# Combining the experts' sums: stores on ScalarE's queue, one addition moved to GpSimd, one semaphore for four loads

## The chip, the cores and the metric

The kernel runs on one core of a Trainium2 chip. The metric is the time of the kernel on the device in microseconds; the time before is 1642.48 us, the median of three runs. All numbers of the trace come from one profiled execution.

## What is computed

One step of a one-layer diffusion trunk on 128 context tokens and 1024 latent tokens of 1024 values: a modulated norm, one projection, linear attention and windowed attention, an output projection with a residual, then a mixture of 64 small experts (8 for each token) with one shared expert, a gated residual and a final norm. The change touches only the end of it:

```
h = silu(einsum('td,edf->tef', xt, wg)) * einsum('td,edf->tef', xt, wu)
routed = einsum('tef,efd->td', h * gates[..., None], wd)
...
xl = xl + g2 * moe(...)          # the gated residual; moe = routed + shared
y_sample = rms_norm(xl, final_norm_g)     # and y_prompt from xc
```

## The kernel before

The program is a row of stages, each in a block of its own, with one instruction stream for each engine: `project`, `linear_attention`, `window_attention`, `out_and_route`, `experts` and `combine`. All values are float32. The 1152 tokens are held as 9 tiles of 128 tokens (`NT`), tile 0 being the context; `x1` keeps the 9 residual tiles of 128x1024 in SBUF from `out_and_route` to the end.

The stage `experts` works in blocks of token rows that share an expert and adds each block's rows into one of two DRAM arrays, `sum_rows0` and `sum_rows1`, each with two halves of rows. So the routed output of a tile is the sum of four 128x1024 blocks in DRAM: `i % 2` picks the array, `i // 2` the half.

The stage `combine` begins when every engine has left `experts`. It handles tile after tile:

- SP issues the four loads of a tile (512 KB each) into `sums[:, t % NB, i, :]`, a ring of `NB` = 6 tiles, in the order 2, 3, 0, 1 (`ARRIVE`), each with a semaphore of its own (L2235). From tile 6 on it first waits until TensorE and DVE are done with the tile that held the slot. After tile 1 it also loads the final norm's weights, `fg`. The stores of the nine results follow in a second loop of the same queue, each after `out_done` (L2241).
- TensorE adds by multiplying with the identity and accumulating in PSUM: all four blocks of the low 512 columns into `ps_low` (L2255), and blocks 0 and 1 of the high 512 columns into `ps_high` (L2252). It takes each load as it comes. A matmul in the code stands as two instructions in the trace.
- VectorE (DVE) adds blocks 2 and 3 of the high columns (L2265), adds `ps_high` to that (L2268), multiplies both halves by the gate row `g2` (L2270, L2272) and adds the product to `x1` (L2274). Then it does the norm of the tile before: the reciprocal (L2280) and the scaling with `rstd` and `fg`, which is written back in place to `x1` (L2282).
- ScalarE (ACT) makes the sum of squares (L2298) and its root (L2300).
- GpSimd (POOL) has nothing to do in this stage.

The order on every engine is the order of the code; nothing reorders it. The set of engines that may read a tile is bounded by the semaphores `low_done`, `g_done`, `x_done`, `ssq_done`, `std_done` and `out_done`.

Of the kernel before, what the change touches and what calls it, by code (L numbers as in the profile page):

```python
# [5 lines left out]
F32 = mybir.dt.float32  # L6
BF16 = mybir.dt.bfloat16
I32 = mybir.dt.int32
ALU = mybir.AluOpType
ACT = mybir.ActivationFunctionType  # L10
AX = mybir.AxisListType

P = 128
D = 1024
KD = D // P
NT = 9
# [20 lines left out]
def cond_of(t):  # L37

    return 0 if t == 0 else 1
# [2157 lines left out]
def combine(nc, dram, keep):  # L2197

    with ExitStack() as ctx:
        def sb(name, shape, dt=F32):  # L2200
            return ctx.enter_context(nc.sbuf_tensor(name, shape, dt))

        def sem(name):
            return nc.alloc_semaphore(name)

        H = D // 2
        NS = 4
        NB = 6
        sums = sb("sums7", [P, NB, NS, D])
        r = [sb(f"r7_{i}", [P, D]) for i in range(2)]  # L2210
        fg = sb("fg", [P, D])
        junk = sb("junk7", [P, D])
        ssq = sb("ssq7", [P, NT])
        std = sb("std7", [P, NT])
        rstd = sb("rstd7", [P, NT])
        ps_low = [ctx.enter_context(nc.psum_tensor(f"ps_low7_{i}", [P, 512], F32)) for i in range(2)]
        ps_high = [ctx.enter_context(nc.psum_tensor(f"ps_high7_{i}", [P, 512], F32)) for i in range(2)]

        sum_in, fg_in = [[sem(f"sum_in{t}_{i}") for i in range(NS)] for t in range(NB)], sem("fg_in")
        ARRIVE = (2, 3, 0, 1)  # L2220
        low_done, high_done, g_done, x_done, ssq_done, std_done, rstd_done, out_done = (
            sem("low7_done"), sem("high7_done"), sem("g7_done"), sem("x7_done"), sem("ssq7_done"), sem("std7_done"), sem("rstd7_done"), sem("out7_done"))
        pair_done = sem("pair7_done")
        stored = sem("stored")
        block = ctx.enter_context(nc.Block())

        @block.sync
        def _(sp):
            for t in range(NT):
                if t >= NB:  # L2230
                    sp.wait_ge(low_done, t - NB + 1)
                    sp.wait_ge(g_done, 2 * (t - NB + 1))  # L2232
                for i in ARRIVE:
                    at = SUM_ROWS * (i // 2) + t * P
                    sp.dma_start(sums[:, t % NB, i, :], dram["y"][i % 2][at:at + P, :]).then_inc(sum_in[t % NB][i], 16)  # L2235
                if t == 1:
                    sp.dma_start(fg[:], dram["final_g"].to_broadcast([P, D])).then_inc(fg_in, 16)  # L2237
            for t in range(NT):

                sp.wait_ge(out_done, t + 1)  # L2240
                sp.dma_start(dram["y_out"](t), keep["x1"][:, t, :]).then_inc(stored, 16)  # L2241
            sp.wait_ge(stored, 16 * NT)

        @block.tensor
        def _(pe):
            for t in range(NT):
                if t >= 2:
                    pe.wait_ge(g_done, 2 * (t - 1))
                for n, i in enumerate(ARRIVE):
                    pe.wait_ge(sum_in[t % NB][i], 16 * (t // NB + 1))  # L2250
                    if i < 2:
                        last = pe.matmul(ps_high[t % 2][:], keep["ident"][:], sums[:, t % NB, i, H:D], start=(i == 0), stop=(i == 1))  # L2252
                    if i == 1:
                        last.then_inc(high_done, 1)
                    last = pe.matmul(ps_low[t % 2][:], keep["ident"][:], sums[:, t % NB, i, 0:H], start=(n == 0), stop=(n == NS - 1))  # L2255
                last.then_inc(low_done, 1)

        @block.vector
        def _(dve):
            def total(t):  # L2260
                s = sums[:, t % NB, :, H:D]
                g2 = keep["g2"][:, cond_of(t), :]
                dve.wait_ge(sum_in[t % NB][2], 16 * (t // NB + 1))
                dve.wait_ge(sum_in[t % NB][3], 16 * (t // NB + 1))
                dve.tensor_tensor(s[:, 2, :], s[:, 2, :], s[:, 3, :], ALU.add).then_inc(pair_done, 1)  # L2265
                dve.wait_ge(high_done, t + 1)
                dve.wait_ge(pair_done, t + 1)
                dve.tensor_tensor(r[t % 2][:, H:D], ps_high[t % 2][:], s[:, 2, :], ALU.add).then_inc(g_done, 1)  # L2268
                dve.wait_ge(low_done, t + 1)
                dve.tensor_tensor(r[t % 2][:, 0:H], ps_low[t % 2][:], g2[:, 0:H], ALU.mult)  # L2270
                dve.wait_ge(g_done, 2 * t + 1)
                dve.tensor_tensor(r[t % 2][:, H:D], r[t % 2][:, H:D], g2[:, H:D], ALU.mult).then_inc(g_done, 1)  # L2272
                dve.wait_ge(g_done, 2 * t + 2)
                dve.tensor_tensor(keep["x1"][:, t, :], keep["x1"][:, t, :], r[t % 2][:], ALU.add).then_inc(x_done, 1)  # L2274

            def norm(t):
                dve.wait_ge(std_done, t + 1)
                if t == 0:
                    dve.wait_ge(fg_in, 16)
                dve.reciprocal(rstd[:, t:t + 1], std[:, t:t + 1]).then_inc(rstd_done, 1)  # L2280
                dve.wait_ge(rstd_done, t + 1)
                dve.scalar_tensor_tensor(out=keep["x1"][:, t, :], in0=keep["x1"][:, t, :], scalar=rstd[:, t:t + 1], in1=fg[:],  # L2282
                                         op0=ALU.mult, op1=ALU.mult).then_inc(out_done, 1)

            for t in range(NT + 1):
                if t < NT:
                    total(t)
                if t >= 1:
                    norm(t - 1)

        @block.scalar
        def _(act):
            nc.scalar.preload_act_table_set("sqrt_and_others")
            for t in range(NT):
                act.wait_ge(x_done, t + 1)
                if t >= 1:
                    act.wait_ge(ssq_done, t)
                act.activation(junk[:], keep["x1"][:, t, :], ACT.Square, accum_out=ssq[:, t:t + 1]).then_inc(ssq_done, 1)  # L2298
                act.wait_ge(ssq_done, t + 1)
                act.activation(std[:, t:t + 1], ssq[:, t:t + 1], ACT.Sqrt, scale=1.0 / D, bias=keep["eps"][:]).then_inc(std_done, 1)  # L2300


def program(nc, dram):
    with ExitStack() as ctx:
# [21 lines left out]
        with ExitStack() as mixer:  # L2326
# [26 lines left out]
            with ExitStack() as late:  # L2353
                def sb(name, shape, dt=F32):
                    return late.enter_context(nc.sbuf_tensor(name, shape, dt))

                keep["tab"] = sb("tab", [P, TAB, 4], I32)
                keep["bexp"] = sb("bexp", [1, 2 * P], I32)
                keep["bend"] = sb("bend", [1, NE + 2], I32)
                keep["g2"] = sb("g2_rows", [P, 2, D])  # L2360
                keep["x1"] = sb("x1", [P, NT, D])
                with nc.sbuf_tensor("h2T", [P, KD, T], F32) as h2T:
                    keep["h2T"] = h2T
                    stage(out_and_route)
                stage(experts)
                stage(combine)
# [78 lines left out]
```

## Time and profile before

| | us |
|---|---|
| median of 3 runs (1638.42 to 1643.2) | 1642.48 |
| the profiled execution itself | 1638.42 |
| its span, first to last instruction | 1636.6 |
| start of `combine`'s first load | 1573.09 |
| TensorE busy, share of the span | 1518.2, 93% |
| DVE busy, share of the span | 719.3, 44% |
| ScalarE busy, share of the span | 530.5, 32% |
| GpSimd busy, share of the span | 543.2, 33% |

The profile's busy times are averages over all stages; this case is read from the last 63 us. The profiled execution is one of the three runs, the fastest; its own time is 1.8 us above its span. A time in a row is counted from the start of the span. PE is TensorE's matmuls, PEld its weight loads, SPq the issuing of DMAs on SP.

### The profile page before, as it was taken

Reading aid. Unit: us, or ns where it says so; the run is one execution under the profiler, and the core shown is the slowest. Engines: PE = TensorE matmul, PEld = TensorE weight load, DVE = VectorE, ACT = ScalarE, POOL = GpSimd, SP = SyncE. Lnnn points to the kernel's source line nnn. Section 1 sums busy time; section 2 is a strip of 40 time slices with the busy share of each in tenths; the row PEclk is TensorE's granted clock in tenths of the full one; section 3 lists DMA queues with packets and bytes.
Section 4 is the critical chain, followed back from the end, with each engine's and each line's share of the span. In section 5 each row is a group of like instructions: output and inputs, shape, how many; then the busy total and the mean of one; then the engine's idle time right before and its main releaser. Section 6 shows DMA issues by size and latency. Waiting matters only on the chain. (4 is left out here: it accounts for less than half of the span.)

```text
span 1636.6 us, 29414 instructions
## 1 busy us (share of the span) xinstructions
PE 1518.2 (93%) x9435; PEld 947.5 (58%) x9436; DVE 719.3 (44%) x1477; ACT 530.5 (32%) x1255; POOL 543.2 (33%) x606
## 2 busy tenths in 40 slices
PE   5999999999899999999999599999999999999757
PEld 2654678787667785555555255555555555555423
DVE  2300144442455553688844244444344444444328
ACT  2400165443156540211100033434333333333312
POOL 0001134344254210111055435555445555544400
PEclk8999999999989999999999799999999999999979
DMA  9991001100283023002000489999999999996569
GB/s 339 348 336 39 20 3 51 46 14 17 74 301 141 9 93 151 39 26 103 14 0 0 165 285 338 333 336 337 345 338 329 335 323 319 257 256 128 77 222 382
DMA packets 107963, 297.42 MB, mean 182 GB/s; under 512 B 12830, under 2 KB 23922, under 8 KB 107634
## 3 DMA queue, kind: packets, MB, share of 16 engines
q1 hardware_dynamic: 81970, 212.54, 34.4%
q0 software_dynamic: 25920, 83.91, 21.2%
q8 instruction: 45, 0.74, 0.2%
q14 instruction: 28, 0.23, 0.0%
HBM read 226.02 MB, written 80.87 MB: 188 GB/s over the span
## 5 line engine op out<-in xcount | busy, mean ns | idle before, releaser
L2080 PE MATMUL ps_g<-w_exp,mix 128*64 x1408 | 326.2, 385 | 6.0 <-DVE own_gu L2175 2.8
L2083 PE MATMUL ps_g<-own_gu,mix 128*64 128x256 f32 x1408 | 326.2, 385 | 0.0
L2080 PEld LDWEIGHTS ps_g<-w_exp,mix 128*64 128x64 f32 x1408 | 187.2, 138 | 107.8 <-issue 11.1
L2083 PEld LDWEIGHTS ps_g<-own_gu,mix 128*64 128x64 f32 x1408 | 187.2, 138 | 0.0
L2029 POOL DMA_INDIRECT sum_rows<-mix,scatter_row x66 | 127.7, 1935 | 171.3 <-DVE mix L2118 145.2
L2052 PE MATMUL ps_y<-w_exp,hidT 128*64 x352 | 171.6, 610 | 6.3 <-ACT own_d L2131 6.3
L2053 PE MATMUL ps_y<-own_d,hidT 128*64 128x512 f32 x352 | 171.6, 610 | 0.0
L511 PE MATMUL ps_f<-late,hT 128*128 128x256 f32 x624 | 144.8, 389 | 0.0
L2175 DVE COPY own_gu<-w_exp 128x2048 f32 x89 | 109.3, 1228 | 65.1 <-issue 43.6
L511 PEld LDWEIGHTS ps_f<-late,hT 128*128 128x128 f32 x624 | 119.8, 195 | 18.7 <-issue 1.9
L1454 PE MATMUL ps_o<-wo,mixT 128*128 128x512 f32 x288 | 125.2, 592 | 0.5 <-DVE h L1707 0.5
L2002 POOL DMA_INDIRECT mix<-h_rows,gather_row x92 | 98.8, 1074 | 78.7 <-POOL gather_row L1999 52.3
L2044 PE MATMUL ps_x<-ident,mix 128*128 128x128 f32 x712 | 103.9, 289 | 14.7 <-DMA mix<-h_rows,gather_row 14.7
L2044 PEld LDWEIGHTS ps_x<-ident,mix 128*128 128x128 f32 x712 | 86.7, 194 | 49.4 <-issue 33.9
L2131 ACT ACTIVATE own_d<-w_exp 128x1024 f32 x88 | 93.3, 1060 | 48.0 <-issue 43.8
L2187 DVE SCALAR_TENSOR_TENSOR hid<-silu,tab,ps_g 128x128 f32<-128x128 f32 x88 | 30.6, 347 | 156.1 <-ACT silu L2152 156.1
L1454 PEld LDWEIGHTS ps_o<-wo,mixT 128*128 128x128 f32 x288 | 54.0, 190 | 65.3 <-issue 65.3
L2118 DVE COPY mix<-ps_y 128x512 f32<-128x512 f32 x66 | 45.7, 692 | 80.2 <-PE ps_y L2053 80.2
L2052 PEld LDWEIGHTS ps_y<-w_exp,hidT 128*64 128x64 f32 x352 | 41.2, 137 | 68.0 <-issue 57.5
L2131 ACT ACTIVATE mix<-ps_x 128x512 f32<-128x512 f32 x89 | 53.2, 598 | 81.2 <-PE ps_x L2044 81.2
L2110 DVE COPY mix<-ps_x 128x512 f32<-128x512 f32 x89 | 61.6, 692 | 39.5 <-PE ps_x L2044 39.5
L1645 POOL TENSOR_TENSOR h<-h,rows 128x1024 f32<-128x1024 f32 x9 | 21.1, 2345 | 156.4 <-DVE h L1714 156.4
(341 smaller groups left out, 2543.7 us busy)
## 6 DMA issues: line engine op xcount, KB each, us to landing
w_exp<-in_exp_w_gate SPq DMA_DIRECT2D x64, 512.0 KB, 7.8
w_exp<-in_exp_w_up SPq DMA_DIRECT2D x64, 512.0 KB, 13.1
w_exp<-in_exp_w_down SPq DMA_DIRECT2D x64, 512.0 KB, 21.4
sum_rows<-mix SPq DMA_DIRECT2D x10, 2048.0 KB, 18.7
sums<-sum_rows SPq DMA_DIRECT2D x36, 512.0 KB, 15.2
ada_ring<-in_w_ada SPq DMA_DIRECT2D x8, 2048.0 KB, 10.7
wring<-in_w_ada SPq DMA_DIRECT2D x3, 2048.0 KB, 12.9
h_rows<-h SPq DMA_DIRECT2D x9, 512.0 KB, 2.6
```

The source lines that it names most:

```text
L511: last = pe.matmul(fill_bank(k), hT[:, j, t * P:(t + 1) * P], keep["late_half"](half)[:, j, :], start=(j == 0), stop=(j == KD - 1))
L1454: last = pe.matmul(ps_o[:, n, :], mixT[t % 2][:, j, :], wo[:, j, n * 512:(n + 1) * 512], start=(j == 0), stop=(j == KD - 1))
L2002: pool.indirect_dma_start(out=x[k], out_offset=None, in_=dram["h2"], in_offset=bass.IndirectOffsetOnAxis(ap=gi[k][:], axis=0), bounds_chec ...
L2029: pool.indirect_dma_start(out=dram["y"][k % 2], out_offset=bass.IndirectOffsetOnAxis(ap=si[k][:], axis=0), in_=y[k], in_offset=None, bound ...
L2044: last = pe.transpose(ps_x[:, j * P:(j + 1) * P], x[k][:, j:D:KD], keep["ident"][:])
L2052: pe.matmul(ps_y[0:HALF, cols], hT[par][:, 0:HALF], w[:, slot * 3 + 2, cols], start=True, stop=True)
L2053: last = pe.matmul(ps_y[HALF:P, cols], hT[par][:, HALF:P], own_d[:, cols], start=True, stop=True)
L2080: pe.matmul(ps_g[par][0:HALF, 0:2 * FF].rearrange("p (k f) -> p k f", k=2), xT[par][:, j * P:j * P + HALF], w[:, bass.ds(slot * 3, 2), ff] ...
L2083: last = pe.matmul(ps_g[par][HALF:P, 0:2 * FF].rearrange("p (k f) -> p k f", k=2), xT[par][:, j * P + HALF:(j + 1) * P], own_gu[par][:, :, ...
L2110: copy(xT[par][:, half * 512:(half + 1) * 512], ps_x[:, half * 512:(half + 1) * 512]).then_inc(done, 1)
L2131: return act.activation(out, in_, ACT.Copy)
L2175: dve.tensor_copy(own_gu[par][:], w[:, bass.ds((e % NW) * 3, 2), :]).then_inc(own_gu_done, 1)
```

## The change

- The loads of a tile come in the order 0, 1, 2, 3 and share one semaphore; TensorE and GpSimd wait for all four.
- TensorE adds the low columns only, in `ps_r`.
- GpSimd gets a block in this stage: for each tile it adds blocks 2 and 3 to blocks 0 and 1 of the high columns in one instruction of 128x2x512, in place. DVE then adds the two results from SBUF.
- The scaled result goes to one of two new tiles `out`, and no longer into `x1`. DVE waits, from tile 2 on, for the store that read that tile.
- The stores are issued by ScalarE, the store of tile t - 1 after the root of tile t, and not by SP after its last load.

```
--- before.py
+++ after.py
@@ -2208,20 +2208,18 @@
         NB = 6
         sums = sb("sums7", [P, NB, NS, D])
         r = [sb(f"r7_{i}", [P, D]) for i in range(2)]
+        out = [sb(f"out7_{i}", [P, D]) for i in range(2)]
         fg = sb("fg", [P, D])
         junk = sb("junk7", [P, D])
         ssq = sb("ssq7", [P, NT])
         std = sb("std7", [P, NT])
         rstd = sb("rstd7", [P, NT])
-        ps_low = [ctx.enter_context(nc.psum_tensor(f"ps_low7_{i}", [P, 512], F32)) for i in range(2)]
-        ps_high = [ctx.enter_context(nc.psum_tensor(f"ps_high7_{i}", [P, 512], F32)) for i in range(2)]
-
-        sum_in, fg_in = [[sem(f"sum_in{t}_{i}") for i in range(NS)] for t in range(NB)], sem("fg_in")
-        ARRIVE = (2, 3, 0, 1)
+        ps_r = [ctx.enter_context(nc.psum_tensor(f"ps_r7_{i}", [P, 512], F32)) for i in range(2)]
+
+        sum_in, fg_in = [sem(f"sum_in{t}") for t in range(NB)], sem("fg_in")
         low_done, high_done, g_done, x_done, ssq_done, std_done, rstd_done, out_done = (
             sem("low7_done"), sem("high7_done"), sem("g7_done"), sem("x7_done"), sem("ssq7_done"), sem("std7_done"), sem("rstd7_done"), sem("out7_done"))
-        pair_done = sem("pair7_done")
-        stored = sem("stored")
+        stored = [sem(f"stored{i}") for i in range(2)]
         block = ctx.enter_context(nc.Block())
 
         @block.sync
@@ -2230,44 +2228,38 @@
                 if t >= NB:
                     sp.wait_ge(low_done, t - NB + 1)
                     sp.wait_ge(g_done, 2 * (t - NB + 1))
-                for i in ARRIVE:
+                for i in range(NS):
                     at = SUM_ROWS * (i // 2) + t * P
-                    sp.dma_start(sums[:, t % NB, i, :], dram["y"][i % 2][at:at + P, :]).then_inc(sum_in[t % NB][i], 16)
+                    sp.dma_start(sums[:, t % NB, i, :], dram["y"][i % 2][at:at + P, :]).then_inc(sum_in[t % NB], 16)
                 if t == 1:
                     sp.dma_start(fg[:], dram["final_g"].to_broadcast([P, D])).then_inc(fg_in, 16)
-            for t in range(NT):
-
-                sp.wait_ge(out_done, t + 1)
-                sp.dma_start(dram["y_out"](t), keep["x1"][:, t, :]).then_inc(stored, 16)
-            sp.wait_ge(stored, 16 * NT)
 
         @block.tensor
         def _(pe):
             for t in range(NT):
+                pe.wait_ge(sum_in[t % NB], 16 * NS * (t // NB + 1))
                 if t >= 2:
                     pe.wait_ge(g_done, 2 * (t - 1))
-                for n, i in enumerate(ARRIVE):
-                    pe.wait_ge(sum_in[t % NB][i], 16 * (t // NB + 1))
-                    if i < 2:
-                        last = pe.matmul(ps_high[t % 2][:], keep["ident"][:], sums[:, t % NB, i, H:D], start=(i == 0), stop=(i == 1))
-                    if i == 1:
-                        last.then_inc(high_done, 1)
-                    last = pe.matmul(ps_low[t % 2][:], keep["ident"][:], sums[:, t % NB, i, 0:H], start=(n == 0), stop=(n == NS - 1))
+                for i in range(NS):
+                    last = pe.matmul(ps_r[t % 2][:], keep["ident"][:], sums[:, t % NB, i, 0:H], start=(i == 0), stop=(i == NS - 1))
                 last.then_inc(low_done, 1)
+
+        @block.gpsimd
+        def _(pool):
+            for t in range(NT):
+                s = sums[:, t % NB, :, H:D]
+                pool.wait_ge(sum_in[t % NB], 16 * NS * (t // NB + 1))
+                pool.tensor_tensor(s[:, 0:2, :], s[:, 0:2, :], s[:, 2:4, :], ALU.add).then_inc(high_done, 1)
 
         @block.vector
         def _(dve):
             def total(t):
                 s = sums[:, t % NB, :, H:D]
                 g2 = keep["g2"][:, cond_of(t), :]
-                dve.wait_ge(sum_in[t % NB][2], 16 * (t // NB + 1))
-                dve.wait_ge(sum_in[t % NB][3], 16 * (t // NB + 1))
-                dve.tensor_tensor(s[:, 2, :], s[:, 2, :], s[:, 3, :], ALU.add).then_inc(pair_done, 1)
                 dve.wait_ge(high_done, t + 1)
-                dve.wait_ge(pair_done, t + 1)
-                dve.tensor_tensor(r[t % 2][:, H:D], ps_high[t % 2][:], s[:, 2, :], ALU.add).then_inc(g_done, 1)
+                dve.tensor_tensor(r[t % 2][:, H:D], s[:, 0, :], s[:, 1, :], ALU.add).then_inc(g_done, 1)
                 dve.wait_ge(low_done, t + 1)
-                dve.tensor_tensor(r[t % 2][:, 0:H], ps_low[t % 2][:], g2[:, 0:H], ALU.mult)
+                dve.tensor_tensor(r[t % 2][:, 0:H], ps_r[t % 2][:], g2[:, 0:H], ALU.mult)
                 dve.wait_ge(g_done, 2 * t + 1)
                 dve.tensor_tensor(r[t % 2][:, H:D], r[t % 2][:, H:D], g2[:, H:D], ALU.mult).then_inc(g_done, 1)
                 dve.wait_ge(g_done, 2 * t + 2)
@@ -2279,7 +2271,10 @@
                     dve.wait_ge(fg_in, 16)
                 dve.reciprocal(rstd[:, t:t + 1], std[:, t:t + 1]).then_inc(rstd_done, 1)
                 dve.wait_ge(rstd_done, t + 1)
-                dve.scalar_tensor_tensor(out=keep["x1"][:, t, :], in0=keep["x1"][:, t, :], scalar=rstd[:, t:t + 1], in1=fg[:],
+                if t >= 2:
+
+                    dve.wait_ge(stored[t % 2], 16 * (t // 2))
+                dve.scalar_tensor_tensor(out=out[t % 2][:], in0=keep["x1"][:, t, :], scalar=rstd[:, t:t + 1], in1=fg[:],
                                          op0=ALU.mult, op1=ALU.mult).then_inc(out_done, 1)
 
             for t in range(NT + 1):
@@ -2291,13 +2286,19 @@
         @block.scalar
         def _(act):
             nc.scalar.preload_act_table_set("sqrt_and_others")
-            for t in range(NT):
-                act.wait_ge(x_done, t + 1)
+            for t in range(NT + 1):
+                if t < NT:
+                    act.wait_ge(x_done, t + 1)
+                    if t >= 1:
+                        act.wait_ge(ssq_done, t)
+                    act.activation(junk[:], keep["x1"][:, t, :], ACT.Square, accum_out=ssq[:, t:t + 1]).then_inc(ssq_done, 1)
+                    act.wait_ge(ssq_done, t + 1)
+                    act.activation(std[:, t:t + 1], ssq[:, t:t + 1], ACT.Sqrt, scale=1.0 / D, bias=keep["eps"][:]).then_inc(std_done, 1)
                 if t >= 1:
-                    act.wait_ge(ssq_done, t)
-                act.activation(junk[:], keep["x1"][:, t, :], ACT.Square, accum_out=ssq[:, t:t + 1]).then_inc(ssq_done, 1)
-                act.wait_ge(ssq_done, t + 1)
-                act.activation(std[:, t:t + 1], ssq[:, t:t + 1], ACT.Sqrt, scale=1.0 / D, bias=keep["eps"][:]).then_inc(std_done, 1)
+                    act.wait_ge(out_done, t)
+                    act.dma_start(dram["y_out"](t - 1), out[(t - 1) % 2][:]).then_inc(stored[(t - 1) % 2], 16)
+            act.wait_ge(stored[0], 16 * 5)
+            act.wait_ge(stored[1], 16 * 4)
 
 
 def program(nc, dram):
```

How a tile stands on DVE, before: its five instructions, then the two of the tile ahead of it (`g_rows` is the gate row, `rstd` the reciprocal root).

```order
L2265 TENSOR_TENSOR sums<-sums 128x512
L2268 TENSOR_TENSOR r_1<-ps_high_1,sums 128x512
L2270 TENSOR_TENSOR r_1<-ps_low_1,g_rows 128x512
L2272 TENSOR_TENSOR r_1<-r_1,g_rows 128x512
L2274 TENSOR_TENSOR x<-x,r_1 128x1024
L2280 RECIPROCAL rstd<-std 128x1
L2282 SCALAR_TENSOR_TENSOR x<-x,rstd,fg 128x1024
```

And the same place on DVE now.

```order
L2260 TENSOR_TENSOR r_1<-sums 128x512
L2262 TENSOR_TENSOR r_1<-ps_r_1,g_rows 128x512
L2264 TENSOR_TENSOR r_1<-r_1,g_rows 128x512
L2266 TENSOR_TENSOR x<-x,r_1 128x1024
L2272 RECIPROCAL rstd<-std 128x1
L2277 SCALAR_TENSOR_TENSOR out_0<-x,rstd,fg 128x1024
```

The addition of blocks 2 and 3 has left DVE, the addition in the second row has both inputs in SBUF, and the last one has another destination.

ScalarE at the end of the program, before (`ssq` is the sum of squares).

```order
L2298 ACTIVATE junk,ssq<-x 128x1024
L2300 ACTIVATE std<-ssq,eps 128x1
L2298 ACTIVATE junk,ssq<-x 128x1024
L2300 ACTIVATE std<-ssq,eps 128x1
L2199 UNCONDITIONAL_BRANCH
```

And now.

```order
L2296 ACTIVATE std<-ssq,eps 128x1
L2299 DMA out_ys<-out_0 128x1024
L2294 ACTIVATE junk,ssq<-x 128x1024
L2296 ACTIVATE std<-ssq,eps 128x1
L2299 DMA out_ys<-out_1 128x1024
L2299 DMA out_ys<-out_0 128x1024
L2199 UNCONDITIONAL_BRANCH
```

A store stands behind each root from tile 1 on, and that of the last tile at the end; on SP the nine stores at the end of its list are gone.

## Rows read from the trace of the kernel before

**Rows 1.** The chain of waits, 1606 to 1637 us; start, duration, what.

```profile
1606.84 16.36 DMA sums<-sum_rows
...
1623.24 1.12 PE ps_high L2252 x2
...
1626.08 0.87 PE ps_low L2255 x2
...
1628.30 1.24 DVE x L2274
...
1631.27 1.28 DVE x L2282
```

**Rows 2.** Stretches; length, busy us and count by engine, PEclk, DMA share, GB/s.

```profile
930.00:940.00 10.00, 4.39 (x20) 3.05 (x22) 3.15 (x3) 0.60 (x1) 2.79 (x4) 0.50 1.03 408
...
1592.00:1598.00 6.00, 6.00 (x15) 2.60 (x14) 5.11 (x8) 1.39 (x4) 0.00 (x0) 1.00 1.03 413
...
1631.00:1632.00 1.00, 0.00 (x0) 0.00 (x0) 0.90 (x2) 0.04 (x1) 0.00 (x0) 0.50 0.41 164
```

**Rows 3.** Instructions in order of time on SP, at its first store.

```profile
1609.20 1.08 SPq L2241 DMA_DIRECT2D out_yp<-x  x1
```

**Rows 4.** The page's DMA issues: the loads; KB each, median us to landing.

```profile
sums<-sum_rows SPq DMA_DIRECT2D x36, 512.0 KB, 15.2
```

**Rows 5.** Line L2241, its nine stores of 512 KB, all from SP.

```profile
DMA to landing us min/median/max: 3.0/15.3/16.1
```

**Rows 6.** Instructions in order of time on TensorE, at the first and last load.

```profile
1576.73 3.48 PE L2255 MATMUL ps_low<-sums,ident 128*128 128x512 f32 x4 [17.50 <-DMA sums<-sum_rows]
...
1624.63 0.19 PEld L2252 LDWEIGHTS ps_high<-sums,ident 128*128 128x128 f32 x1 [0.24 <-DMA sums<-sum_rows]
```

**Rows 7.** The DMA view of 1170 to 1230 us, in the experts' stage.

```profile
q0 software_dynamic: 2305, 7.73, 49.8%
...
w_exp<-in_exp_w_down SPq DMA_DIRECT2D x8, 512.0 KB, 22.1
mix<-h_rows,gather_row POOLq DMA_INDIRECT x9, 8.9
```

**Rows 8.** Groups of instructions, 1560 to 1640 us; busy us, mean ns, idle before.

```profile
L2255 PE MATMUL ps_low<-sums,ident 128*128 128x512 f32 x72 | 36.3, 621 | 17.7 <-DMA sums<-sum_rows 17.5
...
L2282 DVE SCALAR_TENSOR_TENSOR x<-x,rstd,fg 128x1024 f32<-128x1024 f32 x9 | 11.6, 1285 | 0.3
L2274 DVE TENSOR_TENSOR x<-x,r 128x1024 f32<-128x1024 f32 x9 | 11.0, 1225 | 0.3
...
L2268 DVE TENSOR_TENSOR r<-ps_high,sums 128x512 f32<-128x512 f32 x9 | 6.2, 692 | 6.8 <-PE ps_high L2252 6.3
L2270 DVE TENSOR_TENSOR r<-ps_low,g_rows 128x512 f32<-128x512 f32 x9 | 6.2, 686 | 0.7 <-PE ps_low L2255 0.7
L2265 DVE TENSOR_TENSOR sums<-sums 128x512 f32<-128x512 f32 x9 | 6.2, 685 | 18.1 <-DMA sums<-sum_rows 18.1
L2272 DVE TENSOR_TENSOR r<-r,g_rows 128x512 f32<-128x512 f32 x9 | 6.1, 682 | 0.0
...
L2280 DVE RECIPROCAL rstd<-std 128x1 f32<-128x1 f32 x9 | 1.4, 156 | 0.1
```

**Rows 9.** Instructions in order of time on DVE and POOL, in the routing stage.

```profile
842.12 1.22 DVE L1809 TENSOR_TENSOR wo<-iota,rows 128x1024 f32<-128x1024 f32 x1
843.25 1.05 DVE L1807 TENSOR_TENSOR wo<-iota,rows 128x864 f32<-128x864 f32 x1
843.42 2.38 POOL L1651 TENSOR_TENSOR wo<-wo,r_g 128x864 f32<-128x864 f32 x1 [10.48 <-DVE wo L1809]
844.22 2.65 DVE L1809 TENSOR_TENSOR wo<-iota,rows 128x1024 f32<-128x1024 f32 x1
...
848.33 1.62 POOL L1651 TENSOR_TENSOR wo<-wo,r_g 128x864 f32<-128x864 f32 x1
```

**Rows 10.** Groups of instructions on POOL over the whole span.

```profile
L1645 POOL TENSOR_TENSOR h<-h,rows 128x1024 f32<-128x1024 f32 x9 | 21.1, 2345 | 156.4 <-DVE h L1714 156.4
```

## The prediction

> **What bounds the kernel now.** I began with where the change sits. The last stage, `combine`, starts at 1573 us of a 1636.6 us span, so only its 63 us can move. Then the chain of waits, which says what the end hangs on [rows 1]: one load of `sums` in flight for 16.36 us, then one tile's work on TensorE, VectorE and ScalarE, 1623.24 to 1632.55. There is no engine in front of the load, so the load is late because of what was queued ahead of it. The table of stretches confirms that [rows 2]: in the middle of the stage the DMA share is 1.03 at 413 GB/s, and it falls (0.41 in 1631 to 1632) only when the loads are long in and DVE has a last store to finish. The stage is a DMA stream with a tail of compute behind it.
>
> The order of that stream is the point. SP issues its first store at 1609.20 [rows 3], when all 36 loads have been issued. Loads land a median of 15.2 us after issue, stores a median of 15.3 [rows 4, 5]: the stores stand behind the loads. So in the kernel before no store delays a load; the nine stores run while the last tiles are computed, and only the ninth, with nothing ahead of it, is exposed, 3.0 us from issue to landing, the least of the nine [rows 5].
>
> Rate of the stream: the first load has landed at 1576.73, where TensorE starts, and the 35th at 1623.24 [rows 1, 6]. Between them lie 34 transfers of `sums` and the one of `fg`, 35 of 512 KB each in 46.51 us: 1.33 us each, 5.3 us for a tile. The last load of all has landed by 1624.63, where the weight load that waited for it starts [rows 6].
>
> **The change part by part.**
>
> *Stores to ACT's queue, interleaved.* The bytes are the same. But a store of tile t goes out as soon as its `out` is ready, while later loads still wait. If the two queues share the DMA engines, each store that moves before the last load puts that load back by one transfer, 1.33 us. How they share is seen in the experts' stage [rows 7]: GpSimd's gathers of a 512 KB tile land in 8.9 us while the third load of each triple on SP's queue needs 22.1 us, and over these 60 us GpSimd's queue holds 49.8% of the DMA engines' time. So a second queue gets its half at once and does not wait behind the first. A store then moves in about 2 x 1.33 = 2.7 us and lands some 4 to 9 us after issue. The DMA page of the Trainium skill, "DMA: Bandwidth & Descriptors" (Queues, rings and completion order), says the same as a rule, that each DMA engine takes turns between the queues packet by packet; by its opposite, first come first served over all queues, a store would land after 15 us, which is a rival below.
>
> Which stores come before the last load? The tile period becomes at least 5.3 + 1.33 = 6.6 us. The scaled output of tile t is written after the sums of tile t + 1 on DVE, so when DVE keeps up it leaves 3.6 us of TensorE, 2.6 of DVE and 1.5 of scaling after tile t + 1 arrived, about 8; when DVE is held up (next part) it leaves 2.35 + 0.68 + 1.22 + 1.28, about 6, after tile t + 2 arrived. So the stores of tiles 0 to 4 are ahead of the last load, and of tile 5 between none and 0.7. Five stores: 5 x 1.33 = 6.65 us. The last load then lands at 1624.6 + 6.65 = 1631.2.
>
> *The addition on GpSimd.* DVE gives up the pair addition, 685 ns of 5.41 us a tile (the seven DVE rows of [rows 8] added up), and its other addition reads SBUF twice instead of PSUM once (685 against 692 ns: nothing). GpSimd adds 128x1024 values, 2345 ns for as many [rows 10]. Beside DVE it is not free. Rows of the routing stage show it [rows 9]: DVE's L1809 takes 1.22 us alone; when GpSimd's L1651 runs, L1809 takes 2.65 us, and its end moves to that of the GpSimd instruction plus its own 1.2; L1651 itself takes 2.38 instead of 1.63, having started while DVE's L1807 was at work. The two take turns for whole instructions. What they have in common with this stage is two SBUF inputs on DVE. The page "SBUF — State Buffer" of the Trainium skill has this as an exclusive lock between a DVE instruction with two SBUF inputs and a GpSimd instruction that reads SBUF (section "Who interferes with whom"); the rows agree with it. By the rule the two engines need 6.3 us a tile, and without it DVE alone would need 4.7.
>
> So per tile the two share: 2.35 (GpSimd) + 0.69 + 0.68 + 1.22 + 1.28 (DVE's two-input ones) = 6.2 us, and some 0.1 to 0.2 us for what can't be overlapped: about 6.3 us, against 5.41 before and against the 6.6 us of the stream. In the middle of the stage this costs nothing extra, since the stream is slower. At the end it does. At 1631.2, when the last tile arrives, DVE is in the midst of tile 7. Still to come: GpSimd's addition 2.35; tile 7's product 0.68 and sum 1.22; tile 6's output 1.28; then tile 8's 0.69, 0.69, 0.68, 1.22 [rows 8, 10]: 8.8 us, or 8.1 if tile 7's product was already done. I take 8.5. Without turns it would be TensorE's four matmuls, 8 instructions x 0.43 us (half of the last pair, 0.87) plus 0.15, 3.6 us, then 2.6 us as before (1626.95 to 1629.54 [rows 1]): 6.2 us. From the last sum to the end of the span nothing changes: 1636.6 - 1629.54 = 7.1 us [rows 1], with ACT issuing the last store in SP's place.
>
> *TensorE.* 8 instructions a tile (72 in 9 tiles, [rows 8]) and no more the 4 of `ps_high`, so 3.4 us of 6.6 instead of a full engine; it was pacing the stage together with DVE (DMA 5.3, PE 12 x 0.43 = 5.2, DVE 5.4), so its relief buys nothing that the stream doesn't take back. Waiting for all four loads at once puts the last tile 1.3 us later than before (1624.6 against 1623.24); it is counted, since I started from 1624.6.
>
> *The `out` tiles and their wait.* DVE waits for the store of tile t - 2 before it writes tile t's output: two periods, 13 us, less 1.5, against a landing of at most 9: nothing. If it bites, x1's sums queue behind it on DVE, then ScalarE. ACT's issue takes about 1.08 us as on SP [rows 3], with 3 us of idle time there: nothing. SP's loads of tiles 6 to 8 wait for the sums of tiles 0 to 2 as before, with some eleven transfers (15.2 / 1.33) queued ahead that must drain first, so they can be some microseconds late: nothing.
>
> **Sum.** 1631.2 + 8.5 + 7.1 = 1646.8 against 1636.6: +10.2 us; bounds +7.9 (no turns: 6.2 in place of 8.5) and +11.4 (8.8, and 0.7 of tile 5's store ahead of the last load, 0.9). I take +9.8. The profiled execution took 1638.42 us; it is the fastest of the three runs, 4 us under their median 1642.48. Against itself the sum is 1648.2; as a median I expect 1652.3.
>
> **Rivals.**
> 1. *Neither cost is real; not slower.* If stores slip between the loads without delaying them and GpSimd and DVE don't hold each other up, the last tile arrives at 1624.6, TensorE ends 3.6 us later at 1628.2 instead of 1626.95, and the end is +1.2 us: 1643.7. For it: DVE has 0.7 us a tile less. Against: a DMA share of 1.03 leaves no gap for a store [rows 2], and the turns of [rows 9]. It decides only if both fail; one of them alone still costs: DVE and GpSimd at 6.3 us a tile from tile 1's arrival at 1586 put the last sum near 1639 too.
> 2. *Stores stand behind the loads all the same.* Landing 15 us after issue as in [rows 5], then DVE stalls for `stored`: tile 2's output waits 3 us, tile 4's 5 us in all, after which the loads are gone. +5 on the sum: 1657.
> 3. *TensorE's clock.* Working 3.4 us and idle 3.2 it may fall to 0.50 of full speed, which is 1.2 GHz. The stretches of [rows 2] show 0.50 with 4.4 us busy of 10, and 1.00 with a full engine. Four matmuls then take twice 3.44, 6.9 us, and end at A + 7, before DVE wants them in the sum above (A + 5 to 6): 0 to +3.5 us, 1652 to 1656.
> 4. *A gain* would need the earlier stores to shorten the tail by more than they delay loads. The exposed store is the last one, and it needs its 3.0 us in either kernel. I see no more than luck of a fast run.
>
> **How the numbers follow.** Forecast 0.65 (with its own range 1648 to 1655), rival 2 0.1, rival 3 0.1, rival 1 0.1, a gain 0.03, and 0.02 for less than half of the sum. This kernel's runs can tell 0.3% or 4.9 us from no change. Slower than that by forecast and rivals 2 and 3: 0.85; within it 0.11; faster 0.04. The range 1646 to 1658 leaves out most of rival 1 and the far end of rival 2.
>
> **What would show it.** Right: stores from 1597 on among the loads; the wait for the last load ending at 1630 to 1632; DVE's two-input rows with means well above 685, 1225 and 1285 ns or GpSimd's above 2345; TensorE idle in the middle of the stage. Wrong: the last load still at 1625; stores landing 15 us after issue; unstretched rows on both engines; DMA share under 0.9 in mid stage.

## The result and the profile after

The changed kernel takes 1648.17 us, the median of six runs (1645.69 to 1650.57), against 1641.4 us for the kernel before (six runs, 1638.42 to 1643.2). The ratio is 1.0052 with a 95% interval of 1.0039 to 1.0065: slower by half a per cent, or 8.5 us. That ratio is not the quotient of the two medians, which is 1.0041: it rests on more runs than these six, of which the changed kernel has 23 with a median of 1649.61 us. Forecast was 1652.3 against 1642.48, a ratio of 1.006. All ratios here compare fast runs; one run of the kernel with late stores, 1681.03 us, was slow and is not in its ratio.

Both profiled executions lie inside their ranges, but their spans differ by 11.2 us, more than the runs do. 2.8 us of that lie ahead of the place of the change: the first load of `combine` is issued at 1573.09 before and at 1575.84 after, and in the ten experiments below anywhere between 1569.0 and 1578.9, with the same code in front of it. So from here on a stage is timed from its own first load's issue to the end of its span. That gives 63.5 us before and 1647.8 - 1575.84 = 72.0 us after, +8.5.

The same views as [rows 1, 3, 6] for the changed kernel: first pieces of the chain of waits (start, duration, what).

```profile
1575.84 0.33 SPq L2233
...
1595.95 5.41 PE ps_r L2244 x8
...
1604.02 1.23 DVE x L2266
...
1626.74 2.47 DVE r L2264
...
1633.06 2.44 DVE r L2264
...
1636.86 1.28 DVE out L2277
...
1639.98 1.24 DVE x L2266
...
1642.95 1.28 DVE out L2277
```

Where the chain before had one load of 16.36 us in flight and then one tile [rows 1], the chain after runs on DVE from 1601 us on. Its longest pieces there are L2264, a product of 128x512 values that took 682 ns before [rows 8]. The groups of instructions say how often (busy us, mean ns, idle before):

```profile
L2252 POOL TENSOR_TENSOR sums<-sums 128x1024 f32<-128x1024 f32 x9 | 21.5, 2389 | 48.1 <-DMA sums<-sum_rows 48.1
L2264 DVE TENSOR_TENSOR r<-r,g_rows 128x512 f32<-128x512 f32 x9 | 17.0, 1884 | 0.0
...
L2277 DVE SCALAR_TENSOR_TENSOR out<-x,rstd,fg 128x1024 f32<-128x1024 f32 x9 | 13.5, 1496 | 0.3
L2266 DVE TENSOR_TENSOR x<-x,r 128x1024 f32<-128x1024 f32 x9 | 11.0, 1225 | 0.3
...
L2262 DVE TENSOR_TENSOR r<-ps_r,g_rows 128x512 f32<-128x512 f32 x9 | 6.2, 688 | 4.4 <-PE ps_r L2244 4.4
```

L2264 reads SBUF twice and is stretched by 1.2 us on average; L2262, of the same size with one input in PSUM, is not (688 against 686 in [rows 8]). L2266 reads SBUF twice as well and keeps its 1225 ns: GpSimd is not at work when it starts. One tile in order of time, DVE and POOL, shows this:

```profile
1625.46 0.68 DVE L2260 TENSOR_TENSOR r<-sums 128x512 f32<-128x512 f32 x1
1626.06 0.68 DVE L2262 TENSOR_TENSOR r<-ps_r,g_rows 128x512 f32<-128x512 f32 x1
1626.31 2.34 POOL L2252 TENSOR_TENSOR sums<-sums 128x1024 f32<-128x1024 f32 x1 [3.97 <-DMA sums<-sum_rows]
1626.66 2.54 DVE L2264 TENSOR_TENSOR r<-r,g_rows 128x512 f32<-128x512 f32 x1
1629.24 1.22 DVE L2266 TENSOR_TENSOR x<-x,r 128x1024 f32<-128x1024 f32 x1
```

GpSimd starts the moment tile 7 has arrived, 0.35 us ahead of DVE's product for tile 6. It ends at 1628.65 and the product at 1629.20, 0.55 us later, 2.54 us after its own start. L2262 runs across GpSimd's start and takes its usual 0.68.

And the loads. The last tile's matmuls start when all four loads have landed, and ScalarE's issues stand between the squares:

```profile
1632.57 3.70 PE L2244 MATMUL ps_r<-sums,ident 128*128 128x512 f32 x8 [0.89 <-DMA sums<-sum_rows]
```

```profile
1599.82 0.40 ACTq L2299 DMA_DIRECT2D out_yp<-out  x1
...
1625.57 0.34 ACTq L2299 DMA_DIRECT2D out_ys<-out  x1
...
1631.89 0.34 ACTq L2299 DMA_DIRECT2D out_ys<-out  x1
```

The last load lands 56.7 us after the first issue, against 1624.63 - 1573.09 = 51.5 before [rows 6]. Five stores, those of tiles 0 to 4, were issued by 1625.57; the sixth was issued at 1631.89, 0.68 us ahead of the last load's landing, and can have cost it little. The middle of the stage is as full as before: a stretch of six microseconds (length, busy us and count of PE, PEld, DVE, ACT, POOL, then PEclk, DMA share, GB/s).

```profile
1610.00:1616.00 6.00, 3.40 (x6) 1.36 (x5) 5.93 (x7) 1.45 (x3) 2.31 (x1) 0.79 1.02 414
```

### The profile page after: what moved, and what is told of

Read it like the earlier page. It is cut to its first block and busy times, and to the rows that moved or that the text cites. A ratio compares the mean times of both kernels' runs of the same rounds, so it can differ in the third digit from the quotient of the medians.

```text
span 1647.8 us, 29332 instructions
## 1 busy us (share of the span) xinstructions
PE 1510.6 (92%) x9399; PEld 942.9 (57%) x9400; DVE 725.9 (44%) x1468; ACT 530.2 (32%) x1255; POOL 563.8 (34%) x615
## 6 DMA issues: line engine op xcount, KB each, us to landing
wring<-in_w_ada SPq DMA_DIRECT2D x3, 2048.0 KB, 13.1
```

## The experiments

All are counted in the same way; "last load" (its landing, seen by what starts on it) and "last sum" (end of the last sum into x1) are us after the first issue. A stage's time comes from one profiled execution of each kernel; the ratios come from several runs, and where it says one run there is only that one.

| kernel | stage | last load | last sum | ratio to before |
|---|---|---|---|---|
| before | 63.5 | 51.5 | 56.5 | |
| the whole change | 72.0 | 56.7 | 65.4 | 1.0052 [1.0039, 1.0065] |
| stores only | 70.7 | 59.1 | 64.0 | 1.0049 [1.0029, 1.0068] |
| GpSimd and joint wait only | 72.4 | 50.7 | 65.9 | 1.0063 [1.0045, 1.0082] |
| whole, pair on DVE | 69.8 | 56.6 | 63.1 | 1.0044 [1.0032, 1.0057] |
| before, GpSimd adds beside | 76.6 | 51.6 | 69.9 | one run |
| before, GpSimd memset beside | 63.9 | 51.9 | 56.8 | one run |
| stores on ACT, late | 67.2 | 51.9 | 57.0 | 1.0020 [1.0008, 1.0032] |
| `fg` by TensorE | 64.4 | | 57.9 | 1.0014 [1.0003, 1.0025] |
| the same, later | 64.1 | | 57.6 | 1.0014 [0.9999, 1.0029] |
| whole, last two pairs on DVE | 72.2 | 57.7 | 65.6 | one run |
| the same, TensorE filled | 73.2 | 56.4 | 66.5 | one run |

The intervals of the whole change, the stores alone, GpSimd alone and the pair on DVE overlap. The timed runs show that each of the four is slower than the kernel before; the order among them rests on single profiles. In the two kernels with `fg` by TensorE nothing on TensorE or DVE waits for the last load, so its landing can't be read.

**Stores alone.** The store loop leaves SP, and ScalarE gets, at the end of each pass:

```
                 if t >= 1:
+                    act.wait_ge(out_done, t)
+                    act.dma_start(dram["y_out"](t - 1), keep["x1"][:, t - 1, :]).then_inc(stored, 16)
```

> Only the stores are moved to ScalarE's queue (from x1, in place); additions and semaphores are those of the kernel before. Time of the stage is counted from its first load's issue to the end of the span: 63.5 us before, 72.0 us with the whole change. Queue theory (each of five stores puts the last load back by one transfer): the last load lands 56.5 to 58 us after the first issue in place of 51.5, the tail behind it stays 12 us, the stage takes 68.5 to 70 us, +5 to +6.5. Rival (all the loss comes from GpSimd beside DVE): last load at 51.5, stage 63.5 to 64.5.

Measured: stage 70.7 us, +7.2, with every DVE duration as before (means of 684, 1225 and 1285 ns). The last load lands at 59.1 and the stage is longer, both past the ranges I gave. The trace says why. Its weight load, and the store issued last ahead of it:

```profile
1630.13 0.34 ACTq L2299 DMA_DIRECT2D out_ys<-x  x1
```

```profile
1638.04 0.19 PEld L2247 LDWEIGHTS ps_high<-sums,ident 128*128 128x128 f32 x1 [0.24 <-DMA sums<-sum_rows]
```

That is the store of tile 5, the sixth. DVE, not held up by GpSimd, is faster, so six stores get ahead and not five: (59.1 - 51.5) / 6 = 1.27 us a store, and in the whole change (56.7 - 51.5) / 5 = 1.04. The rival, that all the loss is GpSimd's, is out.

**The same queue, but late.** ScalarE waits for the last load before it issues the first store:

```
+                    if t == NT - 2:
+                        act.wait_ge(sum_in[(NT - 1) % NB][1], 32)
+                        for u in range(NT - 2):
+                            act.wait_ge(out_done, u + 1)
+                            act.dma_start(dram["y_out"](u), keep["x1"][:, u, :]).then_inc(stored, 16)
```

> As in the run with the stores alone, all nine stores on ScalarE's queue, but ScalarE waits for the last load to land before it issues the first. Only the time of the stores is changed. Queue theory: the last load lands at 51.5 us after the first issue again, and the stage takes 63.5 to 65.5 us (seven issues of 0.34 us now stand ahead of the last tile's square, partly hidden). If it is the second queue itself or ScalarE's issuing that costs, it stays at 70.7 us.

Measured: the last load is back at 51.9 and the last sum at 57.0.

```profile
1629.83 0.19 PEld L2247 LDWEIGHTS ps_high<-sums,ident 128*128 128x128 f32 x1 [0.24 <-DMA sums<-sum_rows]
```

So it is the time of the stores and not the queue that puts the loads back. The stage takes 67.2, over my range, for a reason of its own:

```profile
1631.41 6.26 ACTq L2301 DMA_DIRECT2D out_ys<-x  x6
```

Six issues in a row took 6.26 us, 1.04 each, where in the changed kernel, a tile apart, they took 0.34 each. The last tile's square stood behind them and DVE waited 2.9 us for its root.

**GpSimd alone.** The whole change with the stores put back on SP behind the loads, from x1:

```
-                    act.dma_start(dram["y_out"](t - 1), out[(t - 1) % 2][:]).then_inc(stored[(t - 1) % 2], 16)
...
+                sp.dma_start(dram["y_out"](t), keep["x1"][:, t, :]).then_inc(stored, 16)
```

> The whole change, but the stores are back on SP behind the loads and the result is written in place in x1, with no wait for a store. Theory of turns (a GpSimd addition and a two-input DVE instruction exclude each other): the last load lands at 51.5 us after the first issue, as before, but DVE and GpSimd need 5.9 to 6.3 us a tile, so the last sum ends near 62 to 65 in place of 56.5 and the stage takes 69 to 72 us, +6 to +8. Rival (only the stores' place costs): +1.2 us for the joint wait, 64.7.

Measured: last load at 50.7, not put back, but stage 72.4, +8.9, and last sum 65.9, both a little over the ranges.

```profile
1629.12 3.20 POOL L2257 TENSOR_TENSOR sums<-sums 128x1024 f32<-128x1024 f32 x1 [2.20 <-DMA sums<-sum_rows]
```

GpSimd's additions start 5.1 us apart now. DVE is slower, so they fall on one instruction after another, and in one tile on two, the scaling and the sum:

```profile
1609.04 2.84 DVE L2265 TENSOR_TENSOR r<-sums 128x512 f32<-128x512 f32 x1
...
1614.44 3.19 DVE L2279 SCALAR_TENSOR_TENSOR x<-x,rstd,fg 128x1024 f32<-128x1024 f32 x1
...
1619.47 3.25 DVE L2271 TENSOR_TENSOR x<-x,r 128x1024 f32<-128x1024 f32 x1
```

Those are 685, 1285 and 1225 ns of work. The rival, that only the stores' place costs, is out too.

**An addition that nobody needs.** To the kernel before, GpSimd adds two scratch blocks of 128x1024 once the last load of each tile has landed:

```
+                pool.wait_ge(sum_in[t % NB][1], 16 * (t // NB + 1))
...
+                pool.tensor_tensor(scr[:, 0, :], scr[:, 0, :], scr[:, 1, :], ALU.add).then_inc(scr_done, 1)
```

> The kernel before, with a GpSimd addition of 128x1024 on two scratch rows for each tile, which nothing in the computation reads or waits for. Theory of turns: DVE's instructions with two SBUF inputs (the pair addition, the product from SBUF, the sum into x1, the scaling) show means above 685, 682, 1225 and 1285 ns, those with a PSUM input stay at 692 and 686, and the stage takes 3 to 6 us more than 63.5. Without turns: all durations as before, 63.5 us.

Measured, the groups of instructions in the stage:

```profile
L2292 DVE SCALAR_TENSOR_TENSOR x<-x,rstd,fg 128x1024 f32<-128x1024 f32 x9 | 15.4, 1707 | 0.3
L2275 DVE TENSOR_TENSOR sums<-sums 128x512 f32<-128x512 f32 x9 | 14.8, 1641 | 17.7 <-DMA sums<-sum_rows 17.7
L2284 DVE TENSOR_TENSOR x<-x,r 128x1024 f32<-128x1024 f32 x9 | 13.0, 1450 | 0.3
L2282 DVE TENSOR_TENSOR r<-r,g_rows 128x512 f32<-128x512 f32 x9 | 7.2, 803 | 0.0
L2278 DVE TENSOR_TENSOR r<-ps_high,sums 128x512 f32<-128x512 f32 x9 | 6.2, 692 | 5.5 <-PE ps_high L2254 4.7
L2280 DVE TENSOR_TENSOR r<-ps_low,g_rows 128x512 f32<-128x512 f32 x9 | 6.1, 681 | 0.2 <-PE ps_low L2257 0.2
```

The split by inputs came out as expected: the four with both inputs in SBUF are longer, the two with a PSUM input are not. The size did not: +13.1 us where I gave 3 to 6. I had added up the time on what the two engines share, 5.9 us a tile. But DVE works in order: while its two-input instruction waits, its one-input ones behind it wait as well. A tile costs DVE its own 5.25 us (most squares of the kernel before start 5.25 apart) and then nearly the 2.35 of the addition: the sums into x1 follow each other in 7.15 to 7.40 us for three tiles that meet one addition each, in 9.42 for one that meets two, and in 5.25 for the last two, when GpSimd is done. The last load lands at 51.6, so none of this is the DMA's.

**The same with a memset.** Two memsets of 128x1024 in place of the addition:

```
+                for n in range(2):
+                    last = pool.memset(scr[:, n, :], 0.0)
```

> The kernel before, with GpSimd writing zeros to 128x2048 scratch values for each tile (two memsets, about 0.9 us each) at the moments where the fourth run had an addition. If what excludes GpSimd and DVE is the reading of SBUF by both, DVE's two-input means stay at 685, 682, 1225 and 1285 ns and the stage at 63.5 us. If any GpSimd work beside DVE costs, the means rise and the stage takes 3 to 8 us more.

Measured: 63.9 us, and

```profile
L2267 POOL MEMSET scr<- 128x1024 f32 x18 | 16.6, 952 | 35.2 <-DMA sums<-sum_rows 35.2
L2294 DVE SCALAR_TENSOR_TENSOR x<-x,rstd,fg 128x1024 f32<-128x1024 f32 x9 | 11.6, 1285 | 0.3
```

with all others unchanged too. GpSimd writing for 1.84 us a tile (16.6 / 9) costs DVE nothing; the addition, which also reads SBUF, costs it.

**The pair on DVE.** The whole change, the instruction moved from GpSimd's block to DVE's:

```
-                pool.tensor_tensor(s[:, 0:2, :], s[:, 0:2, :], s[:, 2:4, :], ALU.add).then_inc(high_done, 1)
...
+                dve.wait_ge(sum_in[t % NB], 16 * NS * (t // NB + 1))
+                dve.tensor_tensor(s[:, 0:2, :], s[:, 0:2, :], s[:, 2:4, :], ALU.add).then_inc(high_done, 1)
```

> The whole change, but GpSimd's instruction is issued on DVE. Theory: DVE needs 4.7 + 1.2 = 5.9 us a tile without turns, less than the stream's 6.3, so the last load stays near 56.7 us and the tail behind it shrinks from 15.2 us to about 13 (TensorE 3.6, DVE 2.6, then 7): stage 69.5 to 70.5 us, 2 us under the whole change. If turns are not what lengthens the tail, it takes 72 us or more, since DVE got longer.

Measured as expected: last load 56.6, stage 69.8, 2.2 us less than the whole change, though DVE has 1.2 us more to do in each tile. The timed ratios of the two, 1.0044 and 1.0052, overlap, so that difference rests on one profile each.

```profile
1632.68 0.30 PEld L2244 LDWEIGHTS ps_r<-sums,ident 128*128 128x128 f32 x2 [3.40 <-DMA sums<-sum_rows]
```

Two things come with it. Six stores were issued ahead of this load and not five (the sixth at 1629.26), so a store cost 0.84 us here, (56.6 - 51.5) / 6. And DVE waited 1.14 us for tile 6's matmuls, which took 5.40 us at a granted clock of 0.72; from there on it runs to its last sum without a wait, so this wait stands in the chain of these 69.8 us.

**Only the last two pairs on DVE.**

```
-            for t in range(NT):
+            for t in range(NT - 2):
...
+                    dve.tensor_tensor(s[:, 0:2, :], s[:, 0:2, :], s[:, 2:4, :], ALU.add).then_inc(pair_done, 1)
```

> The whole change, but for the last two tiles the instruction of GpSimd is issued on DVE. Theory: turns in the middle of the stage are hidden by the stream at 6.3 us a tile and only those at the end cost, so the last load lands at 56.7 us, the tail behind it is about 13.2 us as in the run with all pairs on DVE, and the stage takes 69.5 to 70.5 us. If turns cost all along, it stays near 72 us.

A miss: 72.2 us. DVE, freed of the turn in tile 6, let a sixth store out early, at 1630.71 (last load 57.7), and then TensorE was late. It had idled from 1630.7 on and ran the last tile at a lower granted clock (columns as above):

```profile
1632.00:1634.00 2.00, 0.00 (x0) 0.00 (x0) 1.97 (x4) 0.00 (x0) 0.00 (x0) 0.97 0.63 246
1634.00:1636.00 2.00, 1.83 (x2) 0.83 (x3) 1.96 (x3) 0.96 (x1) 0.00 (x0) 0.50 0.03 10
1636.00:1638.00 2.00, 2.00 (x5) 0.92 (x4) 1.97 (x3) 0.48 (x3) 0.00 (x0) 0.68 0.38 154
```

```profile
1639.43 0.69 DVE L2268 TENSOR_TENSOR r<-ps_r,g_rows 128x512 f32<-128x512 f32 x1 [1.17 <-PE ps_r L2245]
```

0.50 is the level of 1.2 GHz. The four matmuls took 5.2 us, and DVE waited 1.17 us for them.

**The same with TensorE filled.**

```
+                if t < NT - 1:
+                    for n in range(2):
+                        pe.matmul(ps_w[:], keep["ident"][:], keep["g2"][:, 0, 0:H], start=True, stop=True)
```

> As in the run with the last two pairs on DVE, with two more matmuls after each tile but the last, on constants, into a PSUM tile that nobody reads. There TensorE had idled and ran the last tile's four matmuls at 0.50 to 0.68 granted clock in 5.2 us in place of 3.6. Clock theory: the granted clock is 1.00 at the last tile, its matmuls take 3.6 to 3.7 us, the tail behind the last load is 13.2 us in place of 14.4 and the stage takes 70 to 71 us. If the late matmuls had another cause, it stays near 72 us.

The clock part held: 1.00 granted, and the last tile's eight instructions took 3.7 us.

```profile
1625.45 3.70 PE L2246 MATMUL ps_r<-sums,ident 128*128 128x512 f32 x8 [1.76 <-DMA sums<-sum_rows]
```

The stage did not gain: 73.2 us. In this execution GpSimd's turn fell on DVE's scaling (mean 1944 ns, where it was 1495 without the filling) and DVE reached the end of tile 6's sum at 54.6 us and not at 52.9. It also waited 0.48 us for a store. On which instruction the turn falls seems to depend on where DVE stands when a tile lands; between these two single executions it came with a difference of some 2 us.

Do the turns in the middle of the stage cost nothing, as expected here? The rows speak against it. Without DVE's wait of 1.17 us the first of the two stages would have been 71.0 us (an estimate, 72.2 - 1.17), still 1.2 over the 69.8 with no turns at all; and tile 6's sum ended at 52.9 there against 51.7 with all pairs on DVE. How much is hidden stays open, with one execution of each.

**Towards a faster kernel.** The kernel before was not beaten. The idea was a stream shorter by one transfer: the norm's weights as one row of 4 KB, spread by two matmuls, and the last tile's output and store in halves.

```
-                    sp.dma_start(fg[:], dram["final_g"].to_broadcast([P, D])).then_inc(fg_in, 16)
...
+            sp.dma_start(fgrow[:], dram["final_g"]).then_inc(row_in, 16)
...
+                last = pe.matmul(ps_fg[:, n * H:(n + 1) * H], ones[:], fgrow[:, n * H:(n + 1) * H], start=True, stop=True)
```

> The kernel before, with one transfer less in the stream: the final norm's weights come as one row of 4 KB and TensorE spreads them over the partitions; and the last tile's output and store are made in two halves. One transfer is 1.3 us, so the last load should land at 50.2 us; the halves take 0.5 us off the end. Stage 61.5 to 62 us, ratio to the kernel before about 0.999. If the stream were not what sets the end, 63.0 us.

> As in the run with one transfer less, but TensorE spreads the final norm's row after tile 0's matmuls, not ahead of them (there it put tile 0's sum back from 13 to 16 us after the first issue), and ScalarE copies it before tile 1's square. If the kernel before is paced by the stream and by DVE alike (5.25 us a tile each), the last sum ends 55.2 us after the first issue in place of 56.4, the halves take 0.5 us off, and the stage takes 61.5 to 62.3 us, ratio about 0.999. If tile 0's start was not the cause, it stays at 64 us.

Both missed: 64.1 and 64.4 us from the row's issue, ratio 1.0014, where 61.5 to 62.3 was expected. The shorter stream did buy something. From the first sum into x1 to the last it is 41.9 us in the first attempt, against 43.3 before (1585.00 to 1628.30): the sums of tiles 2 and 8 started 6.06 and 5.86 us after the one ahead of them before, and 5.25 now. TensorE lost more at the start. In the first attempt the two matmuls stood ahead of tile 0 at the low clock, 3.78 us at a granted 0.50, and tile 0's sum started late:

```profile
1589.88 1.23 DVE L2291 TENSOR_TENSOR x<-x,r 128x1024 f32<-128x1024 f32 x1
```

That is 14.75 us after the first issue, where it was 11.91 before. In the second attempt they stood behind tile 0, and tile 1's square starts 7.25 us after tile 0's (1588.37 to 1595.62), where before it was 5.15. Most later squares follow each other at 5.25 us in all three kernels. So with 5.2 us a tile for TensorE, 5.25 for DVE and about 5.2 for the stream, one transfer less buys 1.4 us at most, and here it was less than the 2.1 to 2.8 us that TensorE lost.

## Why the prediction was right

- *The stream and the five stores.* Right. Forecast: stores of tiles 0 to 4 ahead of the last load, which moves from 51.5 to 58.1 (1631.2 - 1573.09). Measured 56.7, and exactly those five. A store cost 1.04 us here and not 1.33; in the other kernels with early stores it came to 0.84 to 1.27, each from one execution. My 1.33 was the mean of 35 loads, among them a slow spell at the end; GpSimd's additions in the run without early stores start 5.12 apart, which makes 1.28 a transfer, and in the kernel before tiles 7 and 8 landed 5.94 us apart. That it is the stores' time that does it, the run with late stores shows.
- *The turns of GpSimd and DVE.* Right. Forecast: 8.8 us from the last load to the last sum, or 8.1, taken as 8.5; measured 65.4 - 56.7 = 8.7, the sequence as written. One sign was stated too widely: of DVE's rows with two SBUF inputs those of 685 and 1225 ns kept their means, and what rose was the product (682 to 1884) and the scaling (1285 to 1496), with GpSimd's at 2389. The period of the two engines was to be about 6.3 us against the stream's 6.6; measured, both go at 6.30 (GpSimd's starts at 1613.69, 1619.99, 1626.31), which is what four loads and a store take. By the Trainium skill ("SBUF — State Buffer", Who interferes with whom) a DVE instruction with two SBUF inputs contends with a GpSimd instruction that reads SBUF and not with one that only writes it; the memset run, 63.9 us against 76.6, agrees. "In the middle of the stage this costs nothing extra" is doubtful: see the runs with the last two pairs.
- *From the last sum to the end.* Forecast 7.1, measured 6.6. Probably fewer stores are still in the queue when the last one is issued: it is 6.5 and 6.7 also with the stores on SP where DVE was late (GpSimd alone, GpSimd adding beside), and 7.1 with the memset. No run tests that by itself.
- *Sum.* The terms add up to +10.2; the stage shows +8.5. The stores' price takes 1.4 us of that away and the end 0.5, and the turns give 0.15 back. The forecast +9.8 took 0.4 off the sum without a reason. As a median, 1652.3 was 4.1 us too high: 1.1 of it because the kernel before has 1641.4 in six runs and not 1642.48, 3.0 because the two medians differ by 6.8 and not 9.8. By the ratio of all runs the increase is 8.5. That 1648.17 still fell into the inner range of 1648 to 1655, by 0.17 us, is luck; the direction and both costs are not.
- *Not additive.* The text said that one of the two costs alone would still cost. Stores alone +7.2, GpSimd alone +8.9, both +8.5. A reading of this, not tested by itself: the stores stretch the stream to 6.3 us a tile and so give GpSimd and DVE the time for their turns.
- *Rival 1* (neither cost is real) is out by both single runs. *Rival 2* (stores behind the loads): no DVE wait for a store shows in the changed kernel. The one wait of 0.48 us, with TensorE filled, was for a store that landed 7.9 us after its issue, within the 4 to 9 expected. *Rival 3* (the clock) is true in part: granted 0.79 to 1.00 in mid stage, where before it was 1.00. A tile's matmuls took 5.2 to 5.4 us in mid stage where the clock was low, and not the 6.9 of the text, and the last tile's took 3.70. DVE waited 0.99 us for those of tile 2, which stand in the chain above (5.41); whether that moved the end is open. In two experiments such a wait, of 1.14 and 1.17 us, does stand in the chain's last stretch.
- *One statement was too simple.* "A DMA stream with a tail of compute behind it": the attempts at a shorter stream show that TensorE and DVE pace the stage before nearly as much: 5.25 us from sum to sum, with no wait of DVE between tiles 3 and 7. It took nothing from the sum, since the change made the stream the longer one.

## What to carry to other kernels

When the DMA engines are full up to the last load, stores issued early are not free work done ahead: each puts the last load back, here by 0.84 to 1.27 us where a transfer takes 1.28, and the tail behind that load with it. Behind the loads they fill the time of the last tiles' computation. Before an instruction moves to GpSimd to relieve DVE, look at both operand lists: an addition that reads SBUF there and an instruction with two SBUF inputs here take turns, and since DVE works in order, everything behind the waiting instruction waits too. Two such costs can hide in each other's shadow, so try them one by one: of the 8.5 us, single profiles show 1.3 given back without GpSimd's part, 2.2 with its instruction on DVE, and nothing without the early stores.

## What had not been expected

- Six DMA issues in a row on ScalarE took 6.26 us, 1.04 each, against 0.34 each a tile apart; SP's median in both kernels is 1.04 to 1.05. An issuing engine that also computes pays that.
- A needless GpSimd addition of 2.35 us a tile cost the stage 13.1 us in nine tiles, 1.5 a tile.
- The start of the last stage lay between 1569.0 and 1578.9 us in twelve single executions with the same code before it, about as wide as the whole runs of the kernel before, 1636.7 to 1645.3. Differences of a few microseconds are read within a stage, not from spans.
